# Stick-breaking attention on one core: masks as one float32r product a head, logits of two heads on the two halves of the rows, VectorE's convolution taps in another order

## What is computed

```python
def stick_breaking_attention(q, k, v):
    scale = Dh ** -0.5
    for i in range(S // SB_BLOCK):            # SB_BLOCK = 128, S = 256
        t0, t1 = i * SB_BLOCK, (i + 1) * SB_BLOCK
        z = jnp.einsum('bhqd,bhkd->bhqk', q[:, :, t0:t1], k[:, :, :t1]) * scale
        mask = jnp.arange(t1)[None, :] < jnp.arange(t0, t1)[:, None]
        log_1m = jnp.where(mask, jax.nn.log_sigmoid(-z), 0.0)
        rest = lax.cumsum(log_1m, axis=3, reverse=True) - log_1m
        w = jnp.where(mask, jnp.exp(jax.nn.log_sigmoid(z) + rest), 0.0)
        outs.append(jnp.einsum('bhqk,bhkd->bhqd', w, v[:, :, :t1]))

def even_mixer(h, w_in, w_out, dw_w, dw_b, ln_g, ln_b):
    q, k, v, u, gate = jnp.split(h @ w_in, [512, 1024, 1536, 2048], axis=-1)
    a_out = merge_heads(stick_breaking_attention(heads(q), heads(k), heads(v)))
    c = causal_depthwise_conv(u * jax.nn.sigmoid(gate), dw_w, dw_b)
    c = jax.nn.silu(layer_norm(c, ln_g, ln_b))
    return jnp.concatenate([a_out, c], axis=-1) @ w_out
```

## Time and profile before

| | us |
|---|---|
| median of three runs | 1455.39 (1454.96 to 1455.93) |
| the profiled execution | 1456.73 |
| its span, first to last instruction | 1454.9 |
| TensorE busy in the span | 1425.2 |
| VectorE busy | 946.7 |
| ScalarE busy | 720.1 |
| stage 1 from its first 128x512 product to the last logits | about 202 to 286 |
| the attention, from the first tap on TensorE to the last values | 266.3 to 298.7 |

### The profile page before, as it was taken

How to read it: one execution, slowest core, us unless ns; L and a number is a source line. 1 busy time by engine, 2 the same in 40 slices (tenths; PEclk the granted TensorE clock), 3 DMA queues, 4 the chain that set the end, 5 groups by cost and what they waited for, 6 DMA issues and landing times.

```text
span 1454.9 us, 17894 instructions
## 1 busy us (share of the span) xinstructions
PE 1425.2 (98%) x6715; PEld 1175.4 (81%) x6715; DVE 946.7 (65%) x1323; ACT 720.1 (49%) x1052; POOL 162.5 (11%) x260
## 2 busy tenths in 40 slices
PE   7999999999999999999999999999999999999997
PEld 5888888778888888888878888887877788788886
DVE  5666567687665686675776866755468566755543
ACT  5454355455544355444654545445555734544442
POOL 1900010001000010000162100001443110100000
PEclk9999999999999999999999999999999999999999
DMA  8686765236867768868543488774856445465551
GB/s 270 202 257 207 254 203 202 66 96 203 261 207 251 253 198 257 259 210 267 188 157 123 147 239 245 224 253 138 211 167 195 138 174 173 159 202 174 176 210 64
DMA packets 236342, 286.51 MB, mean 197 GB/s; under 512 B 37028, under 2 KB 160464, under 8 KB 236256
## 3 DMA queue, kind: packets, MB, share of 16 engines
q1 hardware_dynamic: 236000, 285.25, 61.7%
q10 hardware_dynamic: 256, 0.11, 0.0%
HBM read 281.13 MB, written 4.20 MB: 196 GB/s over the span
## 4 chain that ended last, share of the span: by engine, by line
PE 92%; ACT 3%; DVE 2%; issue 1%; POOL 0%; DMA 0%; ACTq 0%; DVEq 0%; POOLq 0%
PE ps L570 28%; PE ps L573 28%; PE ps L571 28%; PE ps L856 2%; PE ps L742 1%; PE ps L1092 1%; ACT whi L459 1%; PE ps L1376 1%; DVE wlo L468 1%; PE ps L1043 0%; PE ps L1016 0%; ACT junk L682 0%; PE ps L994 0%; PE ps L1862 0%; DMA fold<-in_norm_g_dram 0%
## 5 line engine op out<-in xcount | busy, mean ns | idle before, releaser
L468 DVE TENSOR_TENSOR wlo<-raw,whi 128x1024 fp32r<-128x1024 f32 (+2 forms) x474 | 563.1, 1222 | 249.9 <-ACT whi L459 249.3
L459 ACT ACTIVATE whi<-raw 128x1024 fp32r<-128x1024 f32 (+2 forms) x474 | 472.2, 1042 | 245.0 <-PE ps L573 95.2
L570 PE MATMUL ps<-whi,xh 128*128 128x512 f32 (+2 forms) x1440 | 568.3, 395 | 9.3 <-DVE wlo L468 6.8
L571 PE MATMUL ps<-wlo,xh 128*128 128x512 f32 (+2 forms) x1440 | 555.6, 386 | 0.0
L573 PE MATMUL ps<-whi,xl 128*128 128x512 f32 (+2 forms) x1440 | 548.7, 386 | 0.0
L570 PEld LDWEIGHTS ps<-whi,xh 128*128 128x128 f32 x1440 | 271.2, 188 | 68.0 <-DVE wlo L468 9.7
L573 PEld LDWEIGHTS ps<-whi,xl 128*128 128x128 f32 x1440 | 270.8, 188 | 55.6
L571 PEld LDWEIGHTS ps<-wlo,xh 128*128 128x128 f32 x1440 | 271.5, 189 | 50.9
L570 PE MATMUL ps<-whi,gh 128*128 128x512 f32 x440 | 172.6, 392 | 0.0
L571 PE MATMUL ps<-wlo,gh 128*128 128x512 f32 x440 | 171.3, 389 | 0.0
L573 PE MATMUL ps<-whi,gl 128*128 128x512 f32 x440 | 153.5, 389 | 0.0
(11 more groups left out here) (239 smaller groups left out, 926.2 us busy)
## 6 DMA issues: line engine op xcount, KB each, us to landing
raw<-in_ffn_w_in_dram SPq DMA_DIRECT2D x174, 512.0 KB, 5.2
raw<-in_ffn_w_out_dram SPq DMA_DIRECT2D x40, 1024.0 KB, 6.0
raw<-in_w_in_dram SPq DMA_DIRECT2D x26, 1024.0 KB, 5.0
adat<-in_w_ada_dram SPq DMA_DIRECT2D x96, 256.0 KB, 3.0
raw<-in_w_ffn_gate_dram SPq DMA_DIRECT2D x22, 512.0 KB, 4.0
raw<-in_w_ffn_up_dram SPq DMA_DIRECT2D x22, 512.0 KB, 5.1
raw<-in_hyb_w_in_dram SPq DMA_DIRECT2D x10, 1024.0 KB, 5.4
raw<-in_gla_w_in_dram SPq DMA_DIRECT2D x10, 1024.0 KB, 5.6
```

The costliest lines, as they stand in the source:

```text
L459: e.activation(split_of(whi, j), raw_of(j), ACT.Copy).then_inc(*whi_made.up(j))
L468: e.tensor_tensor(split_of(wlo, j), raw_of(j), split_of(whi, j).bitcast(F32), ALU.subtract).then_inc(*wlo_made.up(j))
L570: e.matmul(ps[:, 0:n], a, whi_of(j, k), start=first and k == 0, stop=False)
L571: last = e.matmul(ps[:, 0:n], a, wlo_of(j, k), start=False, stop=False)
```

## The change

Six edits, all in stage 1:

1. A new tile `maskr` in float32r holds the identity and `strict`. ScalarE makes it with two copies of 128x128 (`act_mask`), once, behind the table load L1160 and ahead of the splits of the next four subs.
2. `pe_scores` now takes a pair. For each head one float32r product puts the mask into both strips: its moving operand is the 128 columns of `strict` read twice (`to_broadcast`), its output columns 0 to 127 and 256 to 383.
3. The 256-column products of both heads follow each other, then the 128-column products of both.
4. `NT` goes from 26 to 24: VectorE does two taps fewer (86), TensorE two more (38), one in each of the last two groups of taps.
5. `diag` grows by two blocks, which GpSimd makes.
6. VectorE's order behind `logs(1)`: 26 taps, values 0, logs 2, 6 taps, logs 3, values 1, 8 taps, values 2, the rest. Before it was 14 taps, values 0, 10 taps, logs 2, values 1, 6 taps, logs 3, 12 taps, values 2, the rest.

```diff
--- before.py
+++ after.py
@@ -384,7 +384,7 @@
         with ExitStack() as inner:
             gh = sb("gh", 22 * 256, F32R, where=inner)
             gl = sb("gl", 22 * 256, F32R, where=inner)
-            diag = sb("diag", 36 * P, where=inner)
+            diag = sb("diag", 38 * P, where=inner)
         with ExitStack() as inner:
             cx = sb("cx", 1152, where=inner)[:, 0:4 * 286]
             Y = sb("Y", 4 * 256, where=inner)
@@ -396,6 +396,7 @@
             eb = [sb(f"eb{i}", 384, where=inner) for i in range(4)]
             mb = [sb(f"mb{i}", 384, where=inner) for i in range(4)]
             rb = sb("rb", 512, where=inner)
+            maskr = sb("maskr", 256, F32R, where=inner)
         with ExitStack() as inner:
             gB = sb("gB", 1024, where=inner)
             gQT = sb("gQT", 1024, where=inner)
@@ -947,6 +948,7 @@
         tap_made = sig("tap_made")
         taps_joined = sig("taps_joined")
         scored = sig("scored")
+        mask_made = sig("mask_made")
         abs_made = sig("abs_made")
         exp_made = sig("exp_made")
         ln_made = sig("ln_made")
@@ -964,7 +966,7 @@
         y_scaled = sig("y_scaled")
         y_silu = sig("y_silu")
 
-        NT = 26
+        NT = 24
         PE_TAPS = [(2, k) for k in range(NT, 31)] + [(3, k) for k in range(31)]
         TAPS = [(b, k) for k in range(31) for b in range(3) if b < 2 or k < NT]
         hyb_pair = [(2 * g, 2 * g + 1) for g in range(4)]
@@ -1001,21 +1003,35 @@
         def by_4(z):
             return z[:, :].rearrange("p (b n) -> p b n", b=4)
 
-        def pe_scores(e, hd):
-
-            p0, b = 64 * (hd % 2), hd // 2
-            ps = acc.next(("score", hd), (w_exp, hd))
-            for done in acc.freed:
-                e.wait_ge(*done)
-            if hd % 4 == 0:
-                e.wait_ge(*qk_made.at("q", hd // 4 * 2))
-                e.wait_ge(*qk_made.at("k", hd // 4 * 2))
-            q, k = hqT[p0:p0 + 64, b * 256:(b + 1) * 256], hkT[p0:p0 + 64, b * 256:(b + 1) * 256]
-            e.matmul(ps[:, 0:P], ident, C("strict"), start=True, stop=False, skip_group_check=True)
-            e.matmul(ps[:, 256:384], ident, C("strict"), start=False, stop=False, skip_group_check=True)
-            e.matmul(ps[:, 0:256], k[:, 0:P], q, start=False, stop=True, skip_group_check=True)
-            e.matmul(ps[:, 256:384], k[:, P:256], q[:, P:256], start=False, stop=True,
-                     skip_group_check=True).then_inc(*scored.up(hd))
+        def act_mask(e):
+
+            e.wait_ge(*s_in2.at())
+            e.activation(maskr[:, 0:P], ident, ACT.Copy).then_inc(*mask_made.up(0))
+            e.activation(maskr[:, P:256], C("strict"), ACT.Copy).then_inc(*mask_made.up(1))
+
+        def pe_scores(e, g):
+
+            if g == 0:
+                e.wait_ge(*mask_made.at(1))
+            strict = maskr[:, P:256].rearrange("p (o n) -> p o n", o=1).to_broadcast([P, 2, P])
+            for hd in hyb_pair[g]:
+                ps = acc.next(("score", hd), (w_exp, hd))
+                for done in acc.freed:
+                    e.wait_ge(*done)
+                e.matmul(ps[:, :].rearrange("p (a n) -> p a n", a=2)[:, :, 0:P], maskr[:, 0:P], strict, start=True,
+                         stop=False, skip_group_check=True)
+            if g % 2 == 0:
+                e.wait_ge(*qk_made.at("q", g))
+                e.wait_ge(*qk_made.at("k", g))
+            z = slice(g * 256, (g + 1) * 256)
+            for hd in hyb_pair[g]:
+                r = slice(64 * (hd % 2), 64 * (hd % 2) + 64)
+                e.matmul(acc.of("score", hd)[:, 0:256], hkT[r, z][:, 0:P], hqT[r, z], start=False, stop=True,
+                         skip_group_check=True)
+            for hd in hyb_pair[g]:
+                r = slice(64 * (hd % 2), 64 * (hd % 2) + 64)
+                e.matmul(acc.of("score", hd)[:, 256:384], hkT[r, z][:, P:256], hqT[r, z][:, P:256], start=False,
+                         stop=True, skip_group_check=True).then_inc(*scored.up(hd))
 
         def act_scores(e, hd):
 
@@ -1110,8 +1126,7 @@
                 if i == 1:
                     pe_turn(e, ("k",), hkt, [hyb_qkv.at(3, 0), hyb_qkv.at(3, 1)], hyb_turned, qk_made)
                 if i >= 2:
-                    for hd in hyb_pair[i - 2]:
-                        pe_scores(e, hd)
+                    pe_scores(e, i - 2)
             for c, at in ((2, turn_u), (3, turn_q), (4, turn_k)):
                 pe_chunk(e, 1, j0 + 4 * c, [(hyb_qkv, c, tok) for tok in range(2)], at)
 
@@ -1123,16 +1138,16 @@
             pe_taps(e, PE_TAPS[8:14])
             pair(pe_weights, 1)
             pair(pe_values, 0)
-            pair(pe_scores, 2)
+            pe_scores(e, 2)
             pe_taps(e, PE_TAPS[14:20])
             pair(pe_values, 1)
-            pair(pe_scores, 3)
+            pe_scores(e, 3)
             pe_taps(e, PE_TAPS[20:26])
             pair(pe_weights, 2)
-            pe_taps(e, PE_TAPS[26:31])
+            pe_taps(e, PE_TAPS[26:32])
             pair(pe_weights, 3)
             pair(pe_values, 2)
-            pe_taps(e, PE_TAPS[31:36])
+            pe_taps(e, PE_TAPS[32:38])
             pair(pe_values, 3)
 
             def norm(i):
@@ -1158,6 +1173,7 @@
                              scale=rstd(("h", 1, tok))).then_inc(*hyb_gate.up(tok))
             act_open(e, 1, before, gate)
             e.preload_act_table_set("natural_log_exp_and_others")
+            act_mask(e)
             for i in range(4):
                 act_begin(e, j0 + 4 + i)
             for c in (2, 3, 4):
@@ -1257,14 +1273,13 @@
             logs(0)
             some(5)
             logs(1)
-            some(14)
+            some(26)
             dve_values(e, 0)
-            some(10)
             logs(2)
-            dve_values(e, 1)
             some(6)
             logs(3)
-            some(12)
+            dve_values(e, 1)
+            some(8)
             dve_values(e, 2)
             some(len(TAPS))
             e.wait_ge(*tap_made.at(2, NT - 1))
```

## The result

The changed kernel takes **1449.98 us** (median of 7 runs, 1449.18 to 1453.33), the kernel before 1455.27 (7 runs, 1454.86 to 1455.93). The ratio is 0.9963, 95% interval 0.9954 to 0.9973: 5.4 us less by the ratio, 5.3 by the medians. Forecast were 1449.6 and a gain of 5.8.

What follows compares the result with a forecast made beforehand. TensorE's own queue, busy 98% of the span, was taken as the bound. Four pairs at -6.6 us plus two taps at +0.86 gave -5.8, from 1455.4 to 1449.6 us; range 1448.6 to 1452.2.

Steps and rivals of the forecast that it cites:

- Masks: Attention on TensorE: four fp32 products a pair become two float32r products of 256 columns, 0.118 us each, 0.24 a pair.
- Logits side by side: Attention on TensorE: both heads' products overlap on halves of the rows; entry gap 0.10 us, then 0.87 with exit.
- The index pair: Second block's two heads on rows 0 to 63 and 64 to 127, eight passes in 0.87 us, taken as price.
- The rival of program order: Logits: a pass waits for the start of every pass issued before it; gain only 4.9 us, 1450.5; 5%.
- Four pairs: Masks and logits of the attention's four pairs: 1.66 us saved on each, -6.6 us in all.
- Two taps: Two taps moved from VectorE to TensorE: 2 x 0.431 = +0.86 us on TensorE.
- ScalarE's copies, GpSimd's diagonals: Two copies ahead of the splits and two more diagonals: nothing; without cover the copies cost at most 1.0 us.
- VectorE keeps up: VectorE in the attention: 2.8 us to spare at weights 2, 1.2 to 1.6 at the mean; order worth about 1.
- The sum: Whole kernel: -6.6 + 0.86 = -5.8 us, median 1449.6 us.
- dear forms: Halves one after the other (gain 3.2 us, 1452.2) or masks at fp32's price (gain 3.3, 1452.1); 9%.
- a late VectorE: VectorE or ScalarE becomes the bound late in the stage, TensorE waits 2 us: gain 3.8, 1451.6; 6%.
- late logs 2: Logs 2 come late behind values 0, L1067 and ScalarE; TensorE waits at pair 2; 1458.8 at 12 us delay; 3%.

Runs made afterwards that it cites:

- mask_fp32: The changed kernel with the masks again as two fp32 products of 128 columns a head; 1452.92 us, +2.63 us from first mask to mean.
- apart: The changed kernel with mask and products of one head, then those of the next; 1453.93 us, +4.10 us from first mask to mean.
- head_by_head: The changed kernel with both masks first, then both products of head 0, then those of head 1; 1451.19 us, +0.03 us from first mask to mean.
- taps_30_masks_first_b: The changed kernel with 30 block 2 taps on VectorE, 32 on TensorE, and masks of pairs 2 and 3 ahead of values 0 and 1; 1447.35 us.
- old_order: The changed kernel with VectorE's order behind logs 1 as before the change; 1451.19 us, +0.92 us from first mask to mean.
- taps_26b: The changed kernel with two taps given back to VectorE (26 of block 2 there, 36 on TensorE); 1449.16 us, -0.82 us from first mask to mean.

## Why the prediction was right, step by step

- *Masks* (0.24 a pair): masks and the gap behind them take 0.32 us where 0.34 was forecast. Shown alone by `mask_fp32`: 2.63, expected 2.5.
- *Logits side by side* (0.87 behind the gap at the entry): 254.86 - 254.00 = 0.86 with the exit. The index pair was the right row. Shown by `apart` (4.10, expected 4.2). The rival of program order is refuted by `head_by_head`, 0.03 us where it would be 2.2. A change of form costs near 0.2 us: two fewer saved 0.39 in `taps_30_masks_first_b`. The Trainium skill ("TensorE: Matmul & The Clock Gate", part 3) states that matmuls start and end strictly in program order; between the two halves of the rows these traces do not agree with it. The Trainium skill ("TensorEngine Tiling (Array Packing)", Key Properties) states that a change of mode drains the engine; the 0.39 us agree.
- *Four pairs*, -6.6: 5.91 + 0.86 = 6.77 measured, 0.13 more, since a pair takes 1.18 where 1.21 was forecast.
- *Two taps*, +0.86: the stretch without them is 0.82 shorter.
- *ScalarE's copies, GpSimd's diagonals*: nothing. The copies by the rows above; GpSimd makes the 38 diagonals from 36.33 to 70.42 us, and TensorE first reads one at 261.79. Neither was taken out by itself.
- *VectorE keeps up*: the forecast 2.8 us to spare at weights 2 is 281.07 - 278.33 = 2.7, the idle times are right within 0.1, and the value set on the order, 1.0 us, is 0.92. At the mean the forecast had 1.2 to 1.6 us to spare with two slips that cancel at its upper end: it counted from the end of the last tap (294.6) where the mean needs the step behind it (295.0), and it put the third block 0.4 us behind the mean's start where two products of 0.43 stand between. Measured, L1287 ends at 293.71, 0.8 us before the mean starts and some 1.6 before its third block.
- *The sum*: -5.8 forecast, -5.91 in the stretch, -5.3 by the medians. That the median came within 0.4 us of 1449.6 is in part luck, since a whole time varies by a microsecond that no term of the sum covers (last section). The other rivals (dear forms, a late VectorE, late logs 2) did not come about; `old_order` shows what the last one looks like.

The spans of the two profiled executions differ by 7.2 us, 1.3 more than the change explains. 1.16 of it lies ahead of the first mask and is told below; the rest is 0.13.

## What to carry to other kernels

Where an engine is full, count its passes and its changes between full and half arrays, and take the price from the nearest pair in the same trace: it was right to 0.1 us in 6.8. Products on different halves of the rows overlapped in both orders tried, until one on the full array came between. A faster TensorE shifts the deadlines of the others; follow each queue to its next wait before deciding who gets the leftover work, since here two taps went to the full engine while VectorE still had 1.4 and 3 us gaps.

## What had not been expected

The start of the kernel does not always take the same time, whatever the kernel. TensorE's timeline of before and then of the changed kernel:

```profile
5.30 1.92 PE L742 MATMUL ps<-cst,h 128*128 128x128 f32 x8
...
16.15 0.63 PE L570 MATMUL ps<-whi,xh 128*128 128x512 f32 x1
16.58 0.45 PE L571 MATMUL ps<-wlo,xh 128*128 128x512 f32 x1
16.87 0.40 PE L570 MATMUL ps<-whi,xh 128*128 128x512 f32 x1
...
17.80 1.04 PE L742 MATMUL ps<-cst,h 128*128 128x128 f32 x8
```

```profile
13.81 0.63 PE L572 MATMUL ps<-wlo,xh 128*128 128x512 f32 x1
14.23 0.48 PE L574 MATMUL ps<-whi,xl 128*128 128x512 f32 x1
14.55 0.39 PE L571 MATMUL ps<-whi,xh 128*128 128x512 f32 x1
```

From their first big product at 10.9 and 10.7 us, products of 512 columns start 0.43 us apart; from 16.9 and 14.6 on they start 0.23 apart. TensorE had waited 3.65 us before the first, in both, and was slow before that wait too: the eight matmuls of L742 take 1.92 us at 5.30 and 1.04 at 17.80. Near twice the time is what the lower of TensorE's two clock levels (1.2 and 2.4 GHz) would give, but the granted clock reads 1.00 in all these stretches, so that it was the clock is not shown. The slow stretch is 2.1 us longer in before, which at these paces costs 1.0 us, and its first big product comes 0.2 later: together about the 1.16 us ahead of the first mask.

The slow stretch from the first big product on lasts 3.2 to 3.9 us in three executions (changed, `mask_fp32`, `taps_26b`), whose first mask stands at 253.5 to 253.7 us. In the other seven it lasts 4.9 to 6.0, and the first mask stands at 254.4 to 254.8. So whole times of this kernel carry a microsecond that no edit made; what decides how long the slow stretch lasts stays open.
